# A gated recurrence whose queries are scaled, and whose suffix products are reset, on GpSimd instead of VectorE, with a head's last unit evicted ahead of two decay products

## What is computed

```python
q, k, v, log_f = ...            # per head: 128 keys by 128 values, 4 heads, 528 tokens
for chunk in chunks:            # the reference takes 64 tokens a chunk, the kernel 128
    b = cumsum(log_f)
    o_inter = (q * exp(b)) @ S                      # queries scaled by the decay since the chunk's start
    A = tril(q_t . exp(b_t - b_s) k_s)
    o = o_inter + A @ v
    S = exp(b_last) * S + (k * exp(b_last - b)).T @ v
o = o * rsqrt(mean(o * o) + EPS) * norm_g * silu(g)
```

## Time and profile before

| | |
|---|---|
| median of three runs | 2698.85 us (2694.94 to 2700.21) |
| profiled execution: time, span | 2695.79 us, 2693.9 us |
| busy: PE, DVE, ACT, POOL | 97%, 59%, 41%, 39% of the span |
| the four heads of layer 0 | about 901 to 1048 us of the span |
| the four heads of layer 1 | about 1884 to 2033 us of the span |

### The profile page before, as it was taken

The page is one execution under the profiler, slowest core; times in us unless marked ns, Lnnn a source line. Parts: engine busy times, 40 slices in busy tenths (PEclk is TensorE's granted clock), DMA queues, the critical chain, the costliest instruction groups (busy, mean ns, idle before and its releaser), DMA issues.

```text
span 2693.9 us, 44428 instructions
## 1 busy us (share of the span) xinstructions
PE 2615.2 (97%) x16872; PEld 2318.6 (86%) x16872; DVE 1582.4 (59%) x2486; ACT 1101.7 (41%) x1841; POOL 1052.8 (39%) x675
## 2 busy tenths in 40 slices
PE   7998999999899999999999999999999999999998
PEld 5787788888699998888999999989987777788898
DVE  5665323324489885444476664599884453676665
ACT  4445423323432433433345543323324343454554
POOL 2121444444534222112456544443321124565564
PEclk9999999999999999989999999999999999999999
DMA  5221233232222111101322321222111112332222
GB/s 154 69 80 35 90 101 97 94 93 93 79 72 92 61 58 59 38 26 54 126 87 95 110 95 52 91 92 79 57 55 57 32 40 79 125 104 94 93 102 87
DMA packets 61761, 215.31 MB, mean 80 GB/s; under 512 B 8144, under 2 KB 8144, under 8 KB 61584
## 3 DMA queue, kind: packets, MB, share of 16 engines
q1 hardware_dynamic: 48128, 169.43, 19.8%
q10 hardware_dynamic: 13088, 42.18, 4.7%
q0 software_dynamic: 368, 1.23, 0.2%
HBM read 210.65 MB, written 2.16 MB: 79 GB/s over the span
## 4 chain that ended last, share of the span: by engine, by line
PE 62%; issue 11%; DVE 10%; POOL 5%; POOLq 5%; DVEq 4%; ACT 2%; DMA 0%; ACTq 0%; SPq 0%
PE ps L730 15%; PE ps L731 15%; PE ps L732 15%; POOLq L621 5%; POOL dl L634 3%; PE ps L1186 2%; DVE arena L2021 2%; PE ps L973 1%; PE ps L974 1%; PE ps L975 1%; PE ps L709 1%; PE ps L1161 1%; PE ps L837 1%; POOL wl L619 1%; DVE HID L2021 1%
## 5 line engine op out<-in xcount | busy, mean ns | idle before, releaser
L619 POOL TENSOR_TENSOR wl<-stage,wh 128x512 fp32r<-128x512 f32 (+1 forms) x470 | 807.1, 1731 | 1513.0 <-ACT wh L1326 1512.0
L730 PE MATMUL ps<-Uh,wh 128*128 128x264 f32 (+1 forms) x2624 | 884.7, 337 | 14.1 <-DVE Ul L2027 3.9
L731 PE MATMUL ps<-Ul,wh 128*128 128x264 f32 (+1 forms) x2624 | 854.5, 326 | 0.0
L732 PE MATMUL ps<-Uh,wl 128*128 128x264 f32 (+1 forms) x2624 | 852.8, 325 | 0.0
L1326 ACT ACTIVATE wh<-stage 128x1024 fp32r<-128x1024 f32 x314 | 332.7, 1060 | 835.8 <-PE ps L732 827.4
L730 PEld LDWEIGHTS ps<-Uh,wh 128*128 128x128 f32 x2624 | 497.9, 190 | 71.7 <-issue 17.2
L731 PEld LDWEIGHTS ps<-Ul,wh 128*128 128x128 f32 x2624 | 498.1, 190 | 40.2 <-issue 3.6
L732 PEld LDWEIGHTS ps<-Uh,wl 128*128 128x128 f32 x2624 | 496.2, 189 | 41.3
L2644 DVE SCALAR_TENSOR_TENSOR ps<-arena,v,ps 128x528 f32<-128x528 f32 x232 | 167.8, 769 | 8.3
L634 POOL TENSOR_TENSOR dl<-dstage,dh 128x512 fp32r<-128x512 f32 x112 | 144.6, 1310 | 48.5 <-ACT dh L1422 46.5
L731 PE MATMUL ps<-HIDl,wh 128*128 128x512 f32 (+1 forms) x384 | 137.5, 358 | 0.0
(11 more groups left out here) (377 smaller groups left out, 4926.9 us busy)
## 6 DMA issues: line engine op xcount, KB each, us to landing
stage<-w SPq DMA_DIRECT2D x318, 512.0 KB, 3.5
dstage<-w_down ACTq DMA_DIRECT2D x56, 512.0 KB, 4.3
arena<-bias_rows ACTq DMA_DIRECT2D x16, 448.0 KB, 5.0
arena<-w_mla ACTq DMA_DIRECT2D x8, 384.0 KB, 3.0
H<-xT SPq DMA_DIRECT2D x8, 256.0 KB, 6.9
out<-H ACTq DMA_DIRECT2D x8, 256.0 KB, 2.7
arena<-pT SPq DMA_DIRECT2D x1, 512.0 KB, 8.4
arena<-causal POOLq DMA_DIRECT2D x1, 320.0 KB, 3.9
```

Source lines behind the costliest of these rows:

```text
L619: rest = pool.tensor_tensor(dst[:, cols], stage[:, j, cols], lead[:, cols].bitcast(F32), ALU.subtract)
L730: pe.matmul(dst, w_lead, tok.part(a_lead, h), start=(k == 0), stop=False)
L731: pe.matmul(dst, w_lead, tok.part(a_rest, h), start=False, stop=False)
L732: mm = pe.matmul(dst, w_rest, tok.part(a_lead, h), start=False, stop=(k == len(acts) - 1))
```

## The change

For each head, POOL instead of DVE writes `qfull`, as a tensor_tensor of 128x528, and after it sets `suf` to 1.0 (heads 0 to 2). Both stand in POOL's list of chunks behind the chunk that is split at step 8 of the head and ahead of the one of step 16, behind a wait for `kfull_ready`. PE waits for `qfull_ready` ahead of the head's output products, and DVE for `suf_ready` ahead of the next head's decays. At the end of heads 0 to 2, DVE drains behind `zc` and evicts the output gate's unit ahead of `level_up(BASE)` (level 3) instead of behind it. Two semaphores without use give way to the two new ones.

```diff
+HEADS_FROM = 24
@@ GpSimd's stream, in each layer
-                rest_of_weights(N2_OTHER - KD, PIECES)
+                rest_of_weights(HEADS_FROM + 2, PIECES)
+                done = HEADS_FROM + 2
+                for h in range(HEADS_G):
+                    for chunk in range(done, HEADS_FROM + 4 * h + 3):
+                        rest_of_chunk(chunk % STAGE, PIECES)
+                    done = HEADS_FROM + 4 * h + 3
+                    pool.wait_ge(kfull_ready, n.next(kfull_ready))
+                    pool.tensor_tensor(qfull, qg[h % 2], pre, ALU.mult).then_inc(qfull_ready, 1)
+                    if h < HEADS_G - 1:
+                        pool.memset(suf, 1.0).then_inc(suf_ready, 1)
+                rest_of_chunk(done % STAGE, PIECES)
+                rest_of_weights(N2_OTHER - KD - done - 1, PIECES)
@@ TensorE's stream, recur
                     pe.wait_ge(a_ready, n.next(a_ready))
+                    pe.wait_ge(qfull_ready, n.next(qfull_ready))
                     pe.wait_ge(state_ready, n.next(state_ready))
@@ VectorE's stream, recur(h)
                     times(kfull[:, 0:S], kk[:, 0:S], suf[:, 0:S]).then_inc(kfull_ready, 1)
-                    times(qfull, qg[h % 2], pre)
                     select_pairs(LEVELS - 1)
                     beside(h, 1)
                     select_pairs(LEVELS)
                     dve.drain().then_inc(a_ready, 1)
                     fill(FILL_KEYS)
-                    if following:
-                        dve.memset(suf, 1.0)
                     beside(h, 2)
@@
                     if following:
+                        dve.wait_ge(suf_ready, n.next(suf_ready))
                         prepare_decays()
@@
                         times(zc[:, h, :], oT, gs).then_inc(zc_whole, 1)
+                        dve.drain()
+                    fill(FILL_LAST)
+                    if following:
                         level_up(BASE)
-                    fill(FILL_LAST)
-                    if not following:
+                    else:
                         dve.drain()
                         times(zc[:, h, :], oT, gs).then_inc(zc_whole, 1)
```

More of the change, by code:

```diff
@@ L423, in program @@
         o_free = sem("o_free")
-        r8_ready = sem("r8_ready")
+        qfull_ready = sem("qfull_ready")
         osq_ready = sem("osq_ready")
@@ L488, in program @@
         zb_ready = sem("zb_ready")
-        m_done = sem("m_done")
+        suf_ready = sem("suf_ready")
         d_full = [sem(f"d_full{i}") for i in range(2)]
```

## The result

The changed kernel takes 2756.37 us (median of four runs, 2753.2 to 2758.81), the kernel before 2699.53 us beside it (2694.94 to 2700.67): a ratio of 1.0219, 95% interval 1.0201 to 1.0238. That is 57 us slower, where 4 us faster was forecast. The profiled execution has a span of 2753.5 us, 59.6 us more than before.

The account below looks back on a forecast made before the run. DVE was taken to set the pace between PE's waits, 9.3 us at most. Per layer 1.9 us from the eviction plus 0.2 from the inverse root, over two layers 4.2 us: 2698.85 to 2694.6 us, range 2688.5 to 2700.5.

Parts of the forecast that it names:

- They arrive on POOL: Step placing `qfull` (1.35 us) and memset (0.55 us) on POOL between a head's chunks of steps 8 and 16.
- the new wait costs nothing, with 5 us of cover: PE's wait for `qfull` before the output products: `qfull` done about 956.25, needed after 962, so no loss.
- the slower one: Rival, chance 0.08: port locks pile up mid-head, DVE reaches L2769 1.6 us late, 6.4 us lost in all, 2705 us.
- DVE's lead at L2769: Mid-head, after savings and port locks, DVE between 0.2 us late and 1.3 us early; 0.6 us taken.
- the second rival: Chance 0.16: POOL's locks give back what is taken off and the inverse root comes later; nothing gained, 2698.9 us.
- the assumed place: `qfull` and memset in POOL's list behind the chunk of step 8, about 954.9 to 956.8 in head 1.
- The eviction runs in the shadow of POOL's pieces: At the ends of heads 0 to 2, level 4's operands come 0.62 us sooner, 1.9 us a layer.
- At the change 2 to 3: PE's 1.71 us wait behind the eviction goes; a wait of about 0.4 us at L1027 replaces it.
- The lead of DVE from `qfull` and memset alone: At the head's end, the 1.0 us taken off DVE is spent waiting for POOL's piece; counted as 0.
- it can't use more than 0.85 us of its lead there: At L2769 DVE must wait for PE's update products, ending at 959.4 against L2769's start at 960.29.

Follow-up runs that it names:

- the run with 11: The changed kernel with 11 idle 128x256 matmuls on PE ahead of each wait for `qfull`; ratio 1.0126 to the kernel before.
- eviction alone: The kernel before with only the eviction moved ahead of the level products, `qfull` and memset staying on DVE; ratio 0.9984.
- behind step 8: The changed kernel with POOL's product and memset two chunks sooner, behind the chunk of step 8 instead of step 24; 2695.39 us, ratio 0.9989.
- behind step 16: The changed kernel with POOL's product and memset one chunk sooner, behind the chunk of step 16; ratio 0.9988 to the kernel before.
- step 8, product twice: The changed kernel with POOL's operations two chunks sooner and the product `qfull` made twice, with a drain; ratio 0.9982 to the kernel before.
- step 8, eviction in its old place: The changed kernel with POOL's operations two chunks sooner and the eviction back behind the level products; ratio 1.0008 to the kernel before.
- memset alone in the late place: The changed kernel with `qfull` back on DVE, only the memset on POOL behind the chunk of step 24; ratio 1.0034 to the kernel before.
- the filler of 20: The changed kernel with 20 idle 128x256 matmuls on PE ahead of each wait for `qfull`; ratio 1.0234 to the kernel before.

## Why the prediction was wrong

The loss adds up: 42.8 us of waits for `qfull`, 7.8 us of earlier waits gone, 0.5 us more at later levels (2.0 against 1.5), 25 us for the clock: 42.8 - 7.8 + 0.5 + 25 = 60.5 us, against 57 us in the medians and 59.6 us in the spans.

The runs of one kernel show the clock's part once more. Beside the run with 11 the 28 executions of the kernel before, on the same chip, lie between 2704.22 us at a mean granted clock of 0.982 and 2685.73 us at 0.991; a straight line through all executions there gives 19.2 us for 0.01 (19.3 on the other chip). Most of the spread between executions of one kernel is this. The profiled executions of the two kernels have 0.975 and 0.987: 23 us by that line, and 36.6 of the 59.6 us are left for the waits, which add up to 35.5. The same line, fitted with one level for each kernel, gives the differences at equal clock, an estimate from which a kernel's own effect on the clock drops out (in brackets the 95% interval to either side):

| kernel | PE's waits for DVE and POOL, with filler, against 9.3 us | time against before at equal clock |
|---|---|---|
| eviction alone | -3.5 us | -4.8 us (0.7) |
| behind step 8 | -4.6 us | -4.8 us (0.7) |
| behind step 16 | -4.7 us | -5.8 us (0.7) |
| step 8, product twice | -4.6 us | -5.3 us (0.8) |
| step 8, eviction in its old place | +0.4 us | +0.6 us (0.8) |
| memset alone in the late place | +3.6 us | +4.0 us (0.9) |
| wait filled with 11 | +36.8 us | +36.7 us (1.2) |

The waits account for these times to 1.3 us or better. The plain medians hide it, since they carry the clock's spread.

**The step that failed** is under "They arrive on POOL": "`qfull` lies about 954.9 to 956.25", and from it "the new wait costs nothing, with 5 us of cover". It rests on the sentence of the change that puts `qfull` behind the chunk of step 8. I took a chunk's number in POOL's list for its number in the layer and didn't count what POOL had already taken of the layer when it began. What the runs showed in its place: in the changed kernel `kfull` is done at about 919.1, and `qfull` runs from 931.32 to 932.61, behind a chunk that waits for PE's step 24. A term that the sum has at nothing measured 42.8 us, and the lower clock behind it, which the sum doesn't have at all, 25 us. None of the rivals has this mechanism: the slower one looked for trouble at the port, and I dismissed a late `qfull` by the same wrong place. In the prediction's own sum two figures are off besides, without effect on the outcome: the terms given for DVE's lead at L2769 make 0.2 to 1.5 us early, not 0.2 us late to 1.3 us early, and the range's upper end lies 1.6 us past the second rival, not 1 us.

**Right, and shown.** At the assumed place the working holds by its waits and, at equal clock, by its time (-4.8 us for a forecast of -4.2); the ratio of 0.9989 for a forecast of 0.9984 can't tell it from no change. Its parts:

- The eviction runs in the shadow of POOL's pieces and brings level 4's operands forward. By itself it gives 0.9984 for 3.7 us expected (0.9986), 4.8 us at equal clock. At the change 2 to 3, 0.4 us take the place of 1.7.
- The lead of DVE from `qfull` and memset alone is worth nothing that can be measured: 1.0008, no wait shorter than before.
- The product on POOL takes 1.29 to 1.33 us (1.35 estimated), the memset 0.54 (0.55).
- PE's update products stop DVE at L2769 (L2779 in that file). Forecast was that it can't use more than 0.85 us of its lead there. Counted from the first L1039 of the head, L2779 starts 0.84 us sooner than L2769 did (944.09 to 960.56, against 942.98 to 960.29), behind 0.83 us of waiting. The whole lead was thus 1.67 us, more than the 1.3 us that the forecast had as its most; the limit made that harmless.

**The Trainium skill** ("SBUF — State Buffer", section "Who interferes with whom") says that a VectorE operation with two SBUF inputs contends with a GpSimd operation that reads SBUF and not with one that only writes it. The step 8 run shows both in one row of DVE, head 1 of layer 0:

```profile
959.45 1.13 DVE L2040 SCALAR_TENSOR_TENSOR zal<-arena,zah 128x528 fp32r<-128x528 f32 x1
```

Undisturbed it takes 0.71 us (at 961.68 in that run). It ends at 960.58, 0.57 us behind the end of POOL's product at 960.01, so it waited for the product and ran beside the memset (959.96 to 960.50). The trace agrees with the rule on both counts.

**What stays open.** Whether the work on POOL adds anything to the eviction. The head's period says so (35.8 us in the step 8 run, 36.6 us with the eviction alone), the times hardly do: 0.9989, 0.9988 and 0.9982 against 0.9984, with intervals of 0.0014 to either side. At equal clock the place behind step 8 gives nothing more than the eviction alone (0.1 us, 0.8 to either side), that behind step 16 gives 1.0 us (0.8 to either side). And what decides how long the clock stays low. The version to keep is the eviction alone: within about 1 us of the fastest, with the least change, and 0.16% faster than the kernel before, by an interval that ends at 0.9998.

## What to carry to other kernels

When an operation moves into another engine's queue, write down what stands directly ahead of it there and what that in turn waits for; if the answer is the last step of the engine that will wait for the moved operation, the wait is a full round trip, whatever the operation itself costs. Index a queue's position by what its trace shows (which unit's end releases the instruction ahead), not by a count in the source, since prefetch shifts the count. And before moving work off an engine for its time, look for the wait in which the time is spent anyway: here reordering two operations on the same engine gave all of the gain, or all but 1 us of it.

## What the runs showed of the hardware

Each of the eight waits of 5.2 to 5.7 us on PE was followed at once by half clock, and filling the wait kept the clock at full speed behind all eight. How long it lasts doesn't follow from the wait: behind the same 5.24 us it was 9 us in head 0 of layer 0 and 2.9 us in head 0 of layer 1. Two stretches of 12 us of the changed kernel, from there on (columns as above):

```profile
932.70:944.70 12.00, 11.99 (x69) 11.74 (x70) 6.29 (x10) 3.98 (x7) 0.39 (x1) 0.63 0.10 40
1949.10:1961.10 12.00, 12.00 (x92) 11.85 (x93) 8.80 (x15) 3.98 (x7) 0.35 (x1) 0.88 0.10 39
```

The length of the wait doesn't decide alone whether it comes either. The 1.71 us wait of the earlier trace rows left the matmuls behind it at 0.12 us apart, and in the run with the late memset the six waits of 1.77 us differ: behind two of them came 6.8 us near half clock, behind three 3.4 us, behind one, at 2003.90, none. Ahead of each of the six PE had done the same, twelve one-column matmuls and three projection steps. The first and the last of these six:

```profile
938.20:945.00 6.80, 6.79 (x33) 6.79 (x34) 6.08 (x11) 2.96 (x5) 1.82 (x2) 0.54 0.00 0
2003.90:2010.70 6.80, 6.75 (x42) 5.63 (x43) 6.27 (x10) 2.21 (x3) 3.00 (x2) 1.00 0.00 0
```

A float32 matmul of 128x256 in the filler is recorded as two, 0.22 us each, so the filler of 20 took 8.87 us.
